# Twelve more folded pairs in a feed-forward, with the memory products packed and the token sums on two engines

## The reference

```
x <- LN1(alpha*x + 0.5*SwiGLU_1(x))                          feed-forward 1, inner width 2816
x <- LN2(alpha*x + W_mix_out[conv_group(x) | dsa_group(x)])  projection, conv, sparse attention
x <- LN3(alpha*x + MemCrossAttn(x, mem))                     4 heads, 256 memory tokens
x <- LN4(alpha*x + 0.5*SwiGLU_2(x))                          feed-forward 2
SwiGLU(x) = (silu(x @ w_gate) * (x @ w_up)) @ w_down ;  alpha = 2 ** 0.25
mem_k, mem_v = mem_prompt @ w_mem_k, mem_prompt @ w_mem_v    also outputs
```

## Time and profile before

| | us |
|---|---|
| median of 3 runs | 2498.18 (2497.47 to 2498.34) |
| profiled execution, its time | 2500.18 |
| profiled execution, span | 2498.3 |
| TensorE busy | 2403.2 (96%) |
| GpSimd (POOL) busy | 1299.6 (52%) |
| VectorE (DVE) busy | 1236.4 (49%) |
| ScalarE (ACT) busy | 1080.1 (43%) |
| mean granted TensorE clock | 0.989 of 2.4 GHz |

### The profile page before, as it was taken

The page is one execution under the profiler, slowest core; times in us unless marked ns, Lnnn a source line. Parts: engine busy times, 40 slices in busy tenths (PEclk is TensorE's granted clock), DMA queues, the critical chain, the costliest instruction groups (busy, mean ns, idle before and its releaser), DMA issues.

```text
span 2498.3 us, 40575 instructions
## 1 busy us (share of the span) xinstructions
PE 2403.2 (96%) x15879; PEld 2175.5 (87%) x15879; DVE 1236.4 (49%) x2223; ACT 1080.1 (43%) x2025; POOL 1299.6 (52%) x860
## 2 busy tenths in 40 slices
PE   8999999999999999998999999999989999999998
PEld 8888889888999999987789888888659899899998
DVE  1000002366757566287452689997263436565433
ACT  4333333444545443445543533323463535545341
POOL 4777665543546465422252676766403426556463
PEclk9999999999999999999999999999899999999999
DMA  4444532454233332533121234333502212343322
GB/s 144 122 120 115 162 97 78 137 161 146 79 108 93 93 115 82 156 118 128 34 79 40 69 101 102 110 101 89 171 11 77 60 43 77 112 140 89 116 85 70
DMA packets 427685, 251.85 MB, mean 101 GB/s; under 512 B 23232, under 2 KB 415552, under 8 KB 426224
## 3 DMA queue, kind: packets, MB, share of 16 engines
q1 hardware_dynamic: 389712, 197.88, 27.7%
q10 hardware_dynamic: 35216, 39.38, 4.9%
q0 software_dynamic: 2576, 12.07, 1.3%
HBM read 222.20 MB, written 25.15 MB: 99 GB/s over the span
## 4 chain that ended last, share of the span: by engine, by line
PE 81%; ACT 5%; DVE 5%; POOL 4%; issue 2%; DMA 1%; ACTq 0%; DVEq 0%; POOLq 0%
PE LIN L1052 59%; PE LIN L972 14%; POOL WL L2618 2%; PE TR L1397 1%; PE LIN L1129 1%; ACT WH L1449 1%; POOL XL L2701 1%; PE TR L1105 1%; PE LIN L1345 1%; ACT PR L1995 1%; ACT PT L2020 1%; PE TR L1206 1%; PE TR L1384 1%; DVE SC L2213 1%; DVE PR L2557 1%
## 5 line engine op out<-in xcount | busy, mean ns | idle before, releaser
L2618 POOL TENSOR_TENSOR WL<-WRAW,WH 128x1024 fp32r<-128x1024 f32 (+2 forms) x306 | 715.7, 2344 | 424.6 <-ACT WH L1449 420.5
L1052 PE MATMUL LIN<-XH,WH 128*128 128x256 f32 (+4 forms) x1880 | 601.9, 336 | 21.1 <-DVE Y L2295 6.4
L1052 PE MATMUL LIN<-XL,WH 128*128 128x256 f32 (+4 forms) x1880 | 595.1, 332 | 0.0
L1052 PE MATMUL LIN<-XH,WL 128*128 128x256 f32 (+4 forms) x1880 | 594.6, 332 | 0.0
L1052 PE MATMUL LIN<-HH,WH 128*128 128x256 f32 (+2 forms) x1632 | 465.0, 307 | 1.3 <-POOL HL L2644 0.7
L1052 PE MATMUL LIN<-HL,WH 128*128 128x256 f32 (+2 forms) x1632 | 462.2, 305 | 0.0
L1052 PE MATMUL LIN<-HH,WL 128*128 128x256 f32 (+2 forms) x1632 | 461.4, 305 | 0.0
L1052 PEld LDWEIGHTS LIN<-XH,WH 128*128 128x128 f32 (+1 forms) x1880 | 346.6, 190 | 61.6 <-issue 18.4
L1449 ACT ACTIVATE WH<-WRAW 128x1024 fp32r<-128x1024 f32 (+1 forms) x310 | 318.2, 1028 | 155.6 <-DMA WRAW<-in_ffn_down 52.8
L1052 PEld LDWEIGHTS LIN<-XL,WH 128*128 128x128 f32 (+1 forms) x1880 | 345.8, 189 | 34.1
L1052 PEld LDWEIGHTS LIN<-XH,WL 128*128 128x128 f32 (+1 forms) x1880 | 344.8, 189 | 33.8
(11 more groups left out here) (259 smaller groups left out, 4048.7 us busy)
## 6 DMA issues: line engine op xcount, KB each, us to landing
WRAW<-in_ffn_gate SPq DMA_DIRECT2D x70, 512.0 KB, 3.8
WRAW<-in_ffn_up SPq DMA_DIRECT2D x70, 512.0 KB, 3.8
WRAW<-in_ffn_down SPq DMA_DIRECT2D x64, 512.0 KB, 3.7
WRAW<-in_w_mix_in SPq DMA_DIRECT2D x44, 512.0 KB, 3.8
WRAW<-in_ffn_down SPq DMA_DIRECT2D x32, 384.0 KB, 3.4
WRAW<-in_w_mix_out SPq DMA_DIRECT2D x16, 512.0 KB, 3.7
WRAW<-in_w_mem_q SPq DMA_DIRECT2D x16, 512.0 KB, 3.8
WRAW<-in_w_mem_o SPq DMA_DIRECT2D x16, 512.0 KB, 3.7
```

Source lines behind the costliest of these rows:

```text
L1052: last = pe.matmul(LIN[0:pr.rows, pr.slot, out:out + w], wt[:, SLOT[pr.tile], c, 0:pr.rows], x[:, c, col:col + w], start=(c == 0 and wt is ...
L2618: pool.tensor_tensor(WL[:, SLOT[n], 0:nk, 0:width], raw(n)[:, 0:nk, 0:width], WH[:, SLOT[n], 0:nk, 0:width].bitcast(F32), ALU.subtract).th ...
```

## The change

- `FOLDED` gains `(1, 0)`: in group 0's first feed-forward, the second part keeps four plain whole tiles and makes the other 12 as 6 pairs; the third part makes 6 pairs and keeps its last four tiles.
- The memory products stand one behind each plain tile of the first part (two behind every fourth), and one behind each of its first six down tiles. Turns 0 and 1 follow the keys, 2 and 3 the last two down tiles.
- MKT and MV are stored to DRAM right after they are made, and loaded in group 1's projection as before. The load of the cached memory, its turns and the cached keys come after the second run of pairs. The cached values are loaded after group 1's pairs, not early and kept.
- Group 0's token sums are made from XH and XL, since Y has the first part's down products by then: five operations on VectorE and five on GpSimd of 128x1024 each.
- In all three folded stages VectorE makes sums 0 and 1 and their low parts, GpSimd sums 2 and 3 and theirs.
- In the second feed-forward of group 1 the "scale" strands go. VectorE adds the first part's down products as Y * alpha + product; there ScalarE no longer reads them and GpSimd no longer adds them.
- One semaphore per kept array, and each of the engines waits only for those that it needs.

```diff
-FOLDED = [(1, 1), (2, 1)]
+FOLDED = [(1, 0), (1, 1), (2, 1)]
@@ Plan.stage
-            if between and not halves and whole % 2 == 0:
+            for _ in range(guests(whole) if between and not halves else 0):
@@ Plan.ffn
+            if folded(which, g) and between and split:
+                ups = self.stage("ffn", g, tiles, KD, lambda k: k < RING, between, (0, 1), lambda whole: 1 + (whole % 4 == 0), ...)
+            elif folded(which, g):
+                plain = RING if split or (which, g.index, part) == (1, 0, 1) else 0
@@ fold_strands
-    ffn[RING].mid.append(("fold sums", which, 0))
-    ffn[RING].end.append(("fold sums", which, 1))
+    ffn[RING].mid.append(("fold sums", which))
@@ front, group 0
+            for k in range(2):
+                ffn[turned[KD - 1] + 1 + k].end.append(("memory turn", k))
+                ffn[turned[-1] + 1 + k].end.append(("memory turn", 2 + k))
+            ffn[turned[KD - 1] + 3].end.append(("keep", 4))
+            ffn[turned[-1] + 2].end.append(("keep", 5))
+            assert run[0] == turned[-1] + 7
+            ffn[run[0] - 4].end.append(("fold sums", 1))
+            ffn[run[0] - 2].end.extend([("fold part", 1, 0), ("fold part", 1, 1)])
+            ffn[run[0] - 1].end.extend([("fold part", 1, 2), ("fold part", 1, 3), ("memory stored",)])
+            ffn[run[-1] + 1].mid.append(("memory cache",))
+            for k in range(2):
+                ffn[run[-1] + 4 + k].end.append(("cached memory", k))
+            ffn[run[-1] + 6].end.append(("cached keys",))
@@ back
-            for k in range(KD // 2):
-                ffn[2 * RING + k].end.append(("scale", k))
@@ SP, first loads to WRAWX
+                    if stage_of(IN_PAIR[n]) == 0:
+                        sp.wait_ge(pt_done, 4)
@@ VectorE
+                if two.q == 0 and i == 1:
+                    dve.wait_ge(pt_read, 4)
+                elif pr.kind == "down" and pr.half is None and scaled_late(pr):
+                    dve.scalar_tensor_tensor(y, y, ALPHA, in_psum(pr), ALU.mult, ALU.add).then_inc(product_read[pr.slot], 1)
@@ GpSimd, fold_tokens (group 0; VectorE's has the same form, with TF 0 and 1)
+                    if not g.sample:
+                        pool.wait_ge(moved, memory_moves[0])
+                    for i in range(4) if g.sample else (4, 5):
+                        pool.wait_ge(keep_moved[i], 16)
...
+                        pool.tensor_tensor(TF[:, 2, :, 0:w], XH[:, second, right].bitcast(F32), XH[:, first, right].bitcast(F32),
+                                           ALU.subtract).then_inc(late_step, 1)
+                        more(2, second, right, ALU.add)
+                        more(2, first, right, ALU.subtract)
+                        pool.wait_ge(fold_summed, 2)
+                        pool.tensor_tensor(TF[:, 3, :, 0:w], XH[:, second, left].bitcast(F32), TF[:, 1, :, 0:w], ALU.subtract)\
+                            .then_inc(late_step, 1)
+                        more(3, second, left, ALU.add)
+                        pool.drain().then_inc(fold_late, 2)
@@ GpSimd, the other groups
+                pool.tensor_tensor(TF[:, 2, :, 0:w], Y[:, 4:8, w:2 * w], Y[:, 0:4, w:2 * w], ALU.subtract).then_inc(fold_late, 1)
+                pool.wait_ge(fold_summed, k0 + 2)
+                pool.tensor_tensor(TF[:, 3, :, 0:w], Y[:, 4:8, 0:w], TF[:, 1, :, 0:w], ALU.subtract).then_inc(fold_late, 1)
+            def fold_low(which, k):
+                pool.wait_ge(fold_late, k0 + k - 1)
+                pool.wait_ge(fold_hi, 2 * k0 + k + 1)
+                pool.tensor_tensor(low, full, high, ALU.subtract).then_inc(fold_late_lo, 1)
```

More of the change, by code:

```diff
@@ L206, in add, with stage @@
         return pr
-    def stage(self, name, g, tiles, nk, blocks, between=(), order=(0, 1), **facts):
+    def stage(self, name, g, tiles, nk, blocks, between=(), order=(0, 1), guests=lambda whole: whole % 2 == 0, **facts):
         made, k, whole = [], 0, 0
@@ L263, in ffn @@
             tiles = [((f"ffn{which}_down", P * d, P, f0), d, dict(kind="down", part=part)) for d in range(KD)]
-            downs = self.stage("ffn", g, tiles, nf, lambda k: halves, between, order, which=which,
+            downs = self.stage("ffn", g, tiles, nf, lambda k: halves, between, order, lambda whole: 1, which=which,
                                norm=norm if final else None)
@@ L342, in front @@
             ffn[t - 2].end.append(("load", t))
[L343 removed]
+        run = [k for k, pr in enumerate(ffn) if isinstance(pr, Pair)]
+        if g.sample:
             fold_strands(ffn, g, 1)
[L345 to L346 removed]
+            ffn[run[-1] + 1].mid.append(("cached values",))
+            for i in range(4):
                 ffn[run[-1] + 1 + i].mid.append(("restore", i))
[L348 to L349 removed]
+            for i in (4, 5):
+                mix[4 * i - 3].mid.append(("restore", i))
         if g.index == 1:
@@ L362, in front @@
             ffn[5].end.append(("memory tokens", 1))
-            last = max(k for k, pr in enumerate(ffn) if pr.name == "memkv")
-            for k in range(4):
-                ffn[last + 1 + k].end.append(("memory turn", k))
+            turned = [k for k, pr in enumerate(ffn) if pr.name == "memkv"]
             for k in range(2):
-                ffn[last + 7 + k].end.append(("cached memory", k))
-            ffn[last + 9].end.append(("cached keys",))
+                ffn[turned[KD - 1] + 1 + k].end.append(("memory turn", k))
+                ffn[turned[-1] + 1 + k].end.append(("memory turn", 2 + k))
+                assert not isinstance(ffn[turned[-1] + 1 + k], Pair) and ffn[turned[-1] + 1 + k].kind == "down"
+            ffn[turned[KD - 1] + 3].end.append(("keep", 4))
[8 more added lines that the diff above has]
+            ffn[run[-1] + 6].end.append(("cached keys",))
         mix[1].end.append(("spill residual", 0))
@@ L377, in front @@
         mix[14].end.append(("spill queries",))
-        if not g.sample and folded(1, g1):
-            for i in range(7):
+        if not g.sample:
+            for i in range(4):
                 mix[len(mix) - 8 + i].mid.append(("keep", i))
@@ L551, with scaled_late, added_by @@
 ADDED_AT = {(1, 0): 0, (1, 1): 2 * KD, (2, 0): 4 * KD, (2, 1): 7 * KD}
+def scaled_late(pr):
+    return pr.which == 2 and folded(2, pr.g) and pr.part == 0
+def added_by(which, g, downs):
+    return ADDED_AT[which, g.index] + (max(0, downs - KD) if which == 2 and folded(2, g) else downs)
 EARLY = len(GROUPS[0].tiles)
@@ L2138, in fold @@
                 if two.part:
-                    dve.wait_ge(added, ADDED_AT[two.which, two.g.index] + KD * two.part)
+                    dve.wait_ge(added, added_by(two.which, two.g, KD * two.part))
                 if isinstance(two.before[0], Pair):
@@ L2436, in take_up @@
                     fold_tokens(*what)
-                elif kind == "fold part":
+                elif kind == "fold part" and what[1] < 2:
                     fold_low(*what)
@@ L2707, in take_up @@
                     norm_step(*what)
+                elif kind == "fold sums":
+                    fold_tokens(*what)
+                elif kind == "fold part" and what[1] >= 2:
+                    fold_low(*what)
                 elif kind == "early":
@@ L2744, in consume_ffn @@
                     pool.wait_ge(hidden_lo, pr.event)
-                elif pr.kind == "down" and pr.half is None:
+                elif pr.kind == "down" and pr.half is None and not scaled_late(pr):
                     if pr.part == 0 and pr.j == 0 and pr.which == 2:
```

167 lines of the change are left out of this document (105 added, 62 removed).

## The result

The changed kernel takes 2525.97 us (median of four runs, 2523.17 to 2527.66) against 2498.25 (2497.47 to 2498.34): a ratio of 1.0112 (1.0097 to 1.0127). The sign was forecast, the size was not: +27.7 us where the sum said +6.7, and outside the range.

A forecast was written before the change was run, and what follows sets the result against it. TensorE was taken to bound the kernel, with stops where runs of pairs begin; -13.1 + 11.7 + 1.0 + 1.4 + 5.7 - 2.3 + 2.0 + 0.3 = +6.7 us gave 2505 us, range 2500 to 2510 (8 in 10: 2491 to 2512).

The forecast's parts named there:

- Part 2: Beginning of group 0's run: GpSimd's token sums ahead of the multiply ScalarE awaits delay the third half product, +11.7 us.
- the clock: Beginning of group 0's run: the granted clock may fall to half after the stop; half a fall counted, +1.0 us.
- 37.7: Forecast start in us of group 0's third half product, counted from the first part's last down product, instead of 26.0.
- Part 4: Group 1's two runs, sums split over VectorE and GpSimd: +5.7 us in the second feed-forward, +2.0 in the first.
- the rule: Skill page's shared SBUF port lock: VectorE and GpSimd never overlap; 2506.7 us in all, chance 0.02.
- Part 1: Group 0's first feed-forward: twelve pairs at 10.05 us each replace 24 plain tiles, -13.1 us.
- The ring of PA: Pairs: loop of TensorE, VectorE and ScalarE's copy PA before the third half product, about even with TensorE, 10.05 us.
- rival C: Group 0's pairs: the ring bounds them at 256 columns, 10.35 us a pair, adding 3.6: 2508.5 us; chance 0.13.
- Taken at nothing: Memory products, turns, loads and stores at their new places cost almost nothing: +0.3 us, to 2 at most.
- the ring of four tiles covers six such turns: Group 0's down tiles: buffered tiles cover six 7.2 us weight-buffer turns against TensorE's 4.2 + 2.9; +0.3 us.
- The scaling: Group 1's second feed-forward: without ScalarE scaling Y, three pairs gain 0.76 us each, -2.3 us.
- Part 3: Ends of group 0's two runs: late ScalarE read, and cached memory and key copies before the norm, +1.4 us.

## Why the prediction was wrong in size

The direction was right, and in the main for the reason given: stops in front of the runs, with GpSimd's sums ahead of the multiply that ScalarE awaits, cost more than the pairs save. Not all of them end with PA: of group 0's 16 us, 11.46 end with ScalarE's read of the third plain tile, which stands behind the same multiply, and 3.89 with PA. Five terms of the sum were mis-sized.

**Part 2, +11.7 and +1.0 for the clock; 18.8.** Two steps failed, both ahead of the sums. One is that the copy of the memory values "follows a read and a split and ends at 2.6": the split waited for its load, and the copy ended at 5.1. The other is "the two DMAs land 4.5 and 5.6 us after their issue, so about 9.0": these durations were taken from places where the transfers ran by themselves. Here the two stores and three weight loads are in flight together; the copy that GpSimd waits for landed after 7.5 us, and the pair's up tile after 8.05. The copy and the store are 4.3 of the 7.1 us by which the third half product is later than 37.7, the sums 1.6 and what follows them 1.2. The sums came out near, 18.7 for 17.1, but by luck: of the 6.5 us above 12.2, 5.04 are GpSimd's wait for VectorE's last sum, which the forecast didn't have, and only 1.4 are longer instructions, where it had 4.9. With the products, the turns and the stores moved the term is 14.7, against 12.7 forecast. The clock did fall, to half, within the stop:

```profile
205.00:210.00 5.00, 0.00 (x0) 0.00 (x0) 0.71 (x2) 1.85 (x4) 4.00 (x3) 0.50 0.01 2
```

(columns as in the earlier trace rows: TensorE and its loads did nothing here; the run then begins at 0.65 from 219 to 223.)

**Part 4, how the engines share.** I worked from one row, 3.57 for two VectorE operations and 1.92 and 1.84 on GpSimd, to a rate of sharing: 2.1 us of VectorE cost GpSimd 1.65. The runs show no rate but turns: each instruction waits until the other engine's has ended.

The Trainium skill's page "SBUF — State Buffer", section "SBUF: two separate sides", says just that: a VectorE operation with two SBUF inputs and a GpSimd operation exclude one another for a whole instruction. These traces agree, and with its limit to two SBUF inputs too (0.70 for the sum with an operand in PSUM, 1.43 for 0.69 without). I had given the rule 2 in 100 beside my rate; it should have had the forecast, though its price there, 1.7 us more, would not have saved the sum.

For the second feed-forward the forecast of +5.7 met +6.0 all the same, in part by chance: of the 2.6 us that GpSimd's two sums lose there (2136.11 to 2143.84 for 5.1), 1.23 are a wait for VectorE's second sum.

**Part 1, -13.1; -7.4.** The ring of PA was named, and rival C had its price. What failed is "I estimate that the chain's own shorter operations give back 0.1": the ring holds a VectorE sum that GpSimd's low part doubles at 256 columns. Without that collision a pair takes 9.94, about the forecast's 10.05. Rival C was right that the ring bounds the pairs, and near on the price (10.35; 10.37 over the second run); the member that made the ring long it didn't name. About 1.7 us of the term is the lower clock at the start of the first run, an estimate from 0.65 of full speed from 219 to 223 and 0.92 from 223 to 227.

**Part 4, first feed-forward, +2.0; +7.0.** The change has ScalarE scale the third and fourth sum there (the diff as printed leaves that line out), and I didn't price those two passes (1.12 and 1.09 us). They stand on the chain, and the stop grows from 1.40 to 4.61. Up to the third half product 4.5 us are lost (40.32 from 614.12, against 35.83 from 595.22); the other 2.5 come behind it, where the clock is at half (0.50 from 654.4 to 658).

**Taken at nothing, +0.3; +3.9.** The upper bound of 2 was too low as well. The step that failed is "the ring of four tiles covers six such turns": a turn of 7.2 us against 7.1 of TensorE left nothing for other transfers. Ahead of the first stop, 1.43, a load issued at 117.47 took 7.68 us, with the store of the keys issued at 117.60 (282 GB/s from 120 to 130 us). What made 1.70 the longest of the five isn't separated; all of them went with the products' move.

**The scaling, -2.3; -0.7 to -1.0.** The stops of 0.63 us per pair behind the earlier trace rows are gone, as forecast, but the clock was lower behind the stops in front (0.72 of full speed from 2157 to 2163), where before it had stayed at full.

**Part 3** was +1.4. TensorE's list has two stops there that the kernel before doesn't have, 0.91 at 406.45 and 0.44 at 419.05, 1.35 together; the other 2.2 of the rest up to 614.12 aren't traced.

## What to carry to other kernels

Work split between VectorE and GpSimd isn't done in half the time: count each instruction with two operands in SBUF on both engines as a turn that the other waits out, and keep such turns off any loop that TensorE waits for; here a wait that lets GpSimd start later shortened the pairs, and a reordering of VectorE's list didn't. Price a DMA at the place where it will run, with what is in flight beside it. And when a stop moves instead of going away after a reordering, look for the loop that both places lie on, and shorten its longest member.

## What the runs showed of the hardware

GpSimd and VectorE, each with two operands in SBUF, took turns: 1.23 us became 2.20 or 3.31 and 2.40 became 3.38, one instruction of the other engine at a time, while a VectorE sum with one operand in PSUM kept its 0.70 us beside a GpSimd instruction. Two 1 MB stores beside the weight loads kept the DMA engines full (395 GB/s from 180 to 184 us) and stretched a 3.8 us load to 8.05. And with a stop of 3.01 us in front of the second feed-forward's run the granted clock stayed at full in the kernel before, but was 0.66 of full speed behind the same 3.01 us in the run without pairs in group 0 and with all sums on VectorE: an equal stop doesn't tell whether the clock falls.
